# Half of the output projection moved from its own stage into the waits of the stage before it

## The reference, cut to what matters

```python
y = jnp.concatenate([gla_o, nsa_o], axis=-1) @ w_out      # 1024 x 1024
xp = xp + mod_p[:, 2] * yp                                # residual, gated
hp2 = modulate(xp, g_ffn, mod_p[:, 3], mod_p[:, 4])       # norm, scale, shift
f = moe_ffn(concat([hp2, hs2]), ...)                      # top 4 of 32 experts
y = rmsnorm(xp + mod_p[:, 5] * f, g_final)

def nsa_attend(q, ...):      # compressed, selected and window attention
    imp = sum of compressed softmax -> top_k blocks -> selected softmax
    return gates[0] * o_c + gates[1] * o_s + gates[2] * o_w
```

## Time and profile before

| | us |
|---|---|
| median of the runs | 1851.89 |
| the profiled execution's own time | 1850.02 |
| its span, first to last instruction | 1848.3 |
| sample attention, from barrier to barrier | 461.9 to 543.1 |
| output and router | 543.1 to 668.8 |
| experts and the end | 668.8 to 1848.3 |

### The profile page before, as it was taken

The page is one execution under the profiler, slowest core; times in us unless marked ns, Lnnn a source line. Parts: engine busy times, 40 slices in busy tenths (PEclk is TensorE's granted clock), DMA queues, the critical chain, the costliest instruction groups (busy, mean ns, idle before and its releaser), DMA issues.

```text
span 1848.3 us, 26967 instructions
## 1 busy us (share of the span) xinstructions
PE 1688.6 (91%) x9012; PEld 1314.5 (71%) x9012; DVE 1437.1 (78%) x1353; ACT 1102.1 (60%) x1049; POOL 332.4 (18%) x315
## 2 busy tenths in 40 slices
PE   4999777888779869999999999999999999999994
PEld 2777656555454547888888888888888888888873
DVE  4412464477433768999999999999999999999996
ACT  4221443355332346777777777777777777777772
POOL 0000112300001011222231231231231232222110
PEclk9999979799799869999999999999999999999997
DMA  9454373510046178999999999999999999999973
GB/s 348 167 201 147 82 232 115 168 39 2 14 150 183 64 297 293 356 369 379 374 376 377 377 370 375 380 371 371 387 376 369 388 369 377 384 374 369 388 290 122
DMA packets 112550, 516.08 MB, mean 279 GB/s; under 512 B 25678, under 2 KB 47518, under 8 KB 59754
## 3 DMA queue, kind: packets, MB, share of 16 engines
q1 hardware_dynamic: 99034, 483.48, 69.4%
q0 software_dynamic: 13456, 31.81, 6.1%
HBM read 502.75 MB, written 31.09 MB: 289 GB/s over the span
## 4 chain that ended last, share of the span: by engine, by line
PE 60%; DVE 2%; ACT 1%; DMA 1%; issue 0%; DVEq 0%; POOL 0%; ACTq 0%; POOLq 0%
PE banks L2764 56%; PE banks L2772 3%; PE banks L2750 1%; DMA ffn_rows<-weighed,block_rows 0%; DVE arena L3036 0%; DVE arena L3035 0%; ACT sigmoids L2937 0%; DVE split L2958 0%; PE banks L2822 0%; ACT split L2869 0%; DMA arena<-ffn_rows 0%; DVE arena L3054 0%; DVE split L2962 0%; DVEq L2631 0%; ACT final_stat L2938 0%
## 5 line engine op out<-in xcount | busy, mean ns | idle before, releaser
L2764 PE MATMUL banks<-split 128*128 128x512 f32 x4608 | 1080.0, 394 | 6.9 <-DVE split L2962 5.8
L2764 PEld LDWEIGHTS banks<-split 128*128 128x128 f32 x4608 | 863.3, 189 | 192.9 <-issue 13.7
L2958 DVE TENSOR_TENSOR split<-expert_buffers,split 128x2048 fp32r<-128x2048 f32 x384 | 864.8, 2285 | 44.3 <-ACT split L2869 42.8
L2869 ACT ACTIVATE split<-expert_buffers 128x2048 fp32r<-128x2048 f32 x384 | 733.2, 1918 | 223.6 <-PE banks L2764 216.6
L2703 POOL TENSOR_TENSOR wait_taken<-routing 128x1 f32<-128x1 f32 x62 | 76.1, 1227 | 815.2 <-PE banks L2772 464.4
L2726 POOL DMA_INDIRECT ffn_rows<-weighed,block_rows x31 | 107.7, 3474 | 4.8 <-issue 4.6
L526 PE MATMUL banks<-w_in_high,hT_high 128*128 128x476 f32 x192 | 75.4, 392 | 4.2 <-DVE hT_low L413 4.2
L439 DVE COPY arena<-banks 128x476 f32<-128x476 f32 x12 | 7.8, 654 | 91.1 <-PE banks L526 91.0
L2962 DVE TENSOR_TENSOR split<-banks,split 128x1024 fp32r<-128x1024 f32 x64 | 77.8, 1216 | 0.7 <-ACT split L2872 0.7
L526 PE MATMUL banks<-w_in_high,hT_low 128*128 128x476 f32 x192 | 73.1, 381 | 0.0
L2201 PE MATMUL banks<-arena 128*128 128x512 f32 (+1 forms) x160 | 66.9, 632 | 1.9 <-DMA arena<-in_w_out 1.9
(11 more groups left out here) (391 smaller groups left out, 1688.0 us busy)
## 6 DMA issues: line engine op xcount, KB each, us to landing
expert_buffers<-in_w_gate SPq DMA_DIRECT2D x128, 1024.0 KB, 8.2
expert_buffers<-in_w_up SPq DMA_DIRECT2D x128, 1024.0 KB, 5.9
expert_buffers<-in_w_down SPq DMA_DIRECT2D x128, 1024.0 KB, 9.5
arena<-in_w_ada SPq DMA_DIRECT2D x16, 1024.0 KB, 4.8
w_in_landing<-in_w_in SPq DMA_DIRECT2D x5, 1904.0 KB, 14.3
arena<-in_w_ada SPq DMA_DIRECT2D x4, 2048.0 KB, 22.1
arena<-in_x_prompt SPq DMA_DIRECT2D x8, 512.0 KB, 10.0
arena<-in_cache_cmp POOLq DMA_DIRECT2D x32, 128.0 KB, 3.5
```

The source lines that it names most:

```text
L2764: last = pe.matmul(ps[:, bank + c, :], x[:, kt * P:(kt + 1) * P].bitcast(F32R), wt.bitcast(F32R), start=(m == 2 and kt == 0 and x is xs[0] ...
L2869: act.activation(high[:, j % RING_Q].bitcast(F32R), v, ACT.Copy).then_inc(s_high, 1)
L2958: dve.tensor_tensor(rest[:, j % RING_Q].bitcast(F32R), v, high[:, j % RING_Q], ALU.subtract).then_inc(s_rest, 1)
```

## The change: what it does

Nothing of the arithmetic changes but where and in which order the output projection is computed. Its parts:

- In sample attention TensorE also turns the prompt's mixer rows, in eight groups of four transposes (`turn_mix(g)`), in bank F; ScalarE copies each group back over the rows it came from (`keep_turned(g)`).
- The left half of w_out (columns 0 to 511, 2 MB in 8 loads) is loaded at that stage's start. For each of the four prompt tiles TensorE computes the left half of the projection in two pieces of four slices (`left_half(t, 0, 4)`, `left_half(t, 4, 8)`) in bank F, and ScalarE keeps it in SBUF (`keep_left(t)`).
- The right half (2 MB in 2 loads) is loaded by SyncE in that stage once `values(1)` is done.
- In the output stage `project_out(t)` computes the right half only for the prompt's tiles; the sample tile has both halves there. VectorE's gating of a prompt tile is two operations of 512 columns, not one of 1024. The turning and copying of the prompt rows at its start is gone, and VectorE and ScalarE copy the turned sample rows before their first tile.
- ScalarE issues the stores of the first sums right behind its reads; GpSimd no longer does.
- In `experts`, `overflow` moves from behind `gate(1)` to behind `turn_rows(1)`.
- The sample tile's modulation vectors come in 16 loads, not 8, since their places are split up; other buffers move.

```diff
+    s_wo, s_turned, s_kept, s_yp, s_y = (core.sem(n) for n in (...))
@@ sample attention, SyncE
+            w_out = io["w_out"].rearrange("a (k p) n -> (a p) k n", p=P)
+            for kt in range(KT):
+                sp.dma_start(wout0[kt], w_out[:, kt, 0:512]).then_inc(s_wo, 16)
...
             for i in range(NU):
+                if i == 1:
+                    sp.wait_ge(s_pv, 2)
+                    for a, sem in enumerate(core.s_right):
+                        ks = slice(a * KT // 2, (a + 1) * KT // 2)
+                        sp.dma_start(wout1[:, ks, :], w_out[:, ks, 512:1024]).then_inc(sem, 16)
                 sp.wait_ge(s_res, i + 1)
@@ sample attention, ScalarE
+            def keep_turned(g):
+                t, a = divmod(g, 2)
+                act.wait_ge(s_turned, g + 1)
+                copy(mix[:, t, 512 * a:512 * (a + 1)], ps[:, F, :]).then_inc(s_kept, 1)
+            def keep_left(t):
+                act.wait_ge(s_yp, t + 1)
+                copy(y0[t], ps[:, F, :]).then_inc(s_y, 1)
             turn("k", 0)
+            keep_turned(0)
...
@@ sample attention, TensorE
+            def left_half(t, k0, k1):
+                if k0 == 0:
+                    pe.wait_ge(s_kept, 2 * ST)
+                    if t == 0:
+                        pe.wait_ge(s_wo, 16 * KT)
+                    else:
+                        pe.wait_ge(s_y, t)
+                for kt in range(k0, k1):
+                    last = pe.matmul(ps[:, F, :], mix[:, t, kt * P:(kt + 1) * P], wout0[kt], start=(kt == 0), stop=(kt == KT - 1))
...
+            scores(2)
+            left_half(0, 0, LEFT)
+            turn_weights(1)
+            left_half(0, LEFT, KT)
+            values(1)
+            left_half(1, 0, LEFT)
...
@@ output and router, TensorE
+            def project_out(t):
+                n = TILES[t][1]
                 if t >= 2:
                     pe.wait_ge(s_res, t - 1)
                 for kt in range(KT):
+                    if t == 0 and kt % (KT // 2) == 0:
+                        pe.wait_ge(core.s_right[kt // (KT // 2)], 16)
+                    if kt == KT // 2 and t >= 2:
+                        ranks(t - 2)
+                    right = wout1[:, kt, :]
+                    if t < ST:
+                        last = pe.matmul(ps[:, 4 + t % 2, :], mix[:, t, kt * P:(kt + 1) * P], right, start=(kt == 0), stop=(kt == KT - 1))
@@ output and router, ScalarE, in begin_read
+                act.wait_ge(s_bga, t + 1)
+                act.dma_start(core.ffn_d[t0:t0 + n, :], begin[t][0:n, :]).then_inc(core.s_begun if t else s_first_out, 16)
@@ output and router, VectorE
-                    link(dve.tensor_tensor(hh, ps[0:n, 4 + 2 * (t % 2):6 + 2 * (t % 2), :].rearrange("p b n -> p (b n)"),
-                                           ex[0:n, who, 0, :], ALU.mult))
+                    dve.tensor_tensor(hh[:, 0:512], y0[t], ex_out[0][:, 0:512], ALU.mult)
+                    link(dve.tensor_tensor(hh[:, 512:1024], ps[:, 4 + t % 2, :], ex_out[0][:, 512:1024], ALU.mult))
@@ experts, TensorE
             turn_rows(1, first=True)
+            overflow()
             def step(k, prev, last=False):
                 gate(k, first_of(prev))
-                if is_zero(prev):
-                    overflow()
                 turn_act(k)
```

More of the change, by code:

```diff
@@ L1646, in sample_attention @@
     CMP, IMP = 0, 3 * P
+    core.wout0, core.wout1, core.y0 = output_buffers(core)
+    wout0, wout1, y0 = core.wout0, core.wout1, core.y0
+    core.s_right = [core.sem(f"w_out_right_in{a}", carry=True) for a in range(2)]
+    LEFT = KT // 2
     rounds = [("k", 0, r) for r in range(6)] + [("k", 1, r) for r in range(6)]
@@ L1747, in _ @@
             last.then_inc(s_ec, 1)
+            def keep_turned(g):
[5 more added lines that the diff above has]
+                copy(y0[t], ps[:, F, :]).then_inc(s_y, 1)
             turn("k", 0)
+            keep_turned(0)
             window(0)
+            keep_turned(1)
             turn("k", 1)
+            keep_turned(2)
+            keep_turned(3)
+            keep_turned(4)
             exps(0)
-            for i in range(NU):
-                if i + 1 < NU:
-                    window(i + 1)
-                turn("p", i)
-                if i + 1 < NU:
-                    exps(i + 1)
-                if i + 2 < NU:
-                    turn("k", i + 2)
+            window(1)
+            turn("p", 0)
+            keep_turned(5)
+            exps(1)
+            turn("k", 2)
+            keep_turned(6)
+            keep_turned(7)
+            window(2)
+            turn("p", 1)
+            keep_left(0)
+            exps(2)
+            turn("k", 3)
+            keep_left(1)
+            window(3)
+            turn("p", 2)
+            keep_left(2)
+            exps(3)
+            turn("p", 3)
+            keep_left(3)
         @block.vector
@@ L1944, in _ @@
                       ).then_inc(s_imp, 1)
-            for i in range(NU):
-                if i + 1 < NU:
-                    scores(i + 1)
-                turn_weights(i)
-                if i + 2 < LATE:
-                    keys(i + 2)
-                values(i)
-                if LATE <= i + 2 < NU:
-                    keys(i + 2)
+            turn_mix(3)
+            turn_mix(4)
+            scores(1)
+            turn_weights(0)
+            turn_mix(5)
+            keys(2)
+            turn_mix(6)
+            values(0)
+            turn_mix(7)
+            scores(2)
[4 more added lines that the diff above has]
+            left_half(1, 0, LEFT)
+            keys(3)
+            left_half(1, LEFT, KT)
+            scores(3)
+            left_half(2, 0, LEFT)
+            turn_weights(2)
+            left_half(2, LEFT, KT)
+            values(2)
+            left_half(3, 0, LEFT)
+            turn_weights(3)
+            values(3)
+            left_half(3, LEFT, KT)
 def routing_tables(core):
@@ L2006, in output_and_router @@
     core.z_moe = own.at
-    mixT = own.take(KT * NTOK).rearrange("p (k n) -> p k n", k=KT)
-    wout = own.take(KT * D).rearrange("p (k n) -> p k n", k=KT)
+    own.take(KT * NTOK + KT * D)
+    hole = [core.pf + 2 * D + i * DIN + 512 for i in range(3)]
+    wout0, wout1, y0 = core.wout0, core.wout1, core.y0
+    mixST = mix[:, ST, 0:KT * (NTOK - SEQ)].rearrange("p (k n) -> p k n", k=KT)
     gate2 = core.gate2
@@ L2026, in output_and_router @@
     h2 = own.take(2 * D).rearrange("p (u n) -> p u n", u=2)
-    own = Stack(core, late.at, core.z1)
-    ex = own.take(6 * D).rearrange("p (w v n) -> p w v n", w=2, v=3)
+    own = Stack(core, late.at, core.z1 - 2 * PAST // PAGE * 256)
+    ex_out = [core.arena[:, hole[0] + 512:hole[0] + 512 + D], own.take(D)]
+    ex_ffn = [core.arena[:, at:at + 2 * D].rearrange("p (v n) -> p v n", v=2) for at in hole[1:3]]
     h2T = own.take(KT * P).rearrange("p (k n) -> p k n", k=KT)
@@ L2126, in _ @@
                     sp.wait_ge(s_yp, NT)
+                    sp.wait_ge(s_bp, 1)
                     for i in range(LANDING):
@@ L2162, in _ @@
             gather_rows(core, pool)
-            for t in range(2, NT):
-                store_begin(t)
             pool.wait_ge(s_bo, 16)
```

126 lines of the change are left out of this document (62 added, 64 removed).

## The result

Five runs of the changed kernel took 1833.33 to 1840.26 us, median **1835.73 us**; five of the kernel before, 1848.33 to 1853.65, median 1851.89. The ratio is 0.9924, 95% interval 0.9905 to 0.9943: 14 us less, between 10.6 and 17.6 (the two medians are 16.2 us apart). The profiled run's span went from 1848.3 to 1834.0 us.

A forecast was written before the change was run, and what follows sets the result against it. TensorE, busy 91% of the span, bounds the kernel; only waits, lower clock or movable work can give time. 19.7 - 28.6 - 1.0 - 2.3 = -12.2 us, from 1851.89 to a median of 1839.7; 8 in 10: 1829 to 1853.

The forecast's parts named there:

- the likeliest case: Whole kernel: the forecast itself, a median of 1839.7 us within 1834 to 1845, chance 0.58.
- sample attention: Sample attention: added pieces and transposes, partly in TensorE's holes, start the next stage +19.7 us later, bounds +14 and +26.
- output stage to the sample tile: Output stage up to VectorE's start on the sample tile: halved projections give -28.6 us, bounds -32.5 and -9.
- tail: End of the output stage: ScalarE's stores replace GpSimd's before the barrier, -1 us, bounds +1 and -4.
- `overflow`: Experts' stage: moved, it starts in a hole of 2.38 us and delays the gate by 2.3: -2.3 us.
- The forecast's 4.3: Sample attention from 504.73 to the stage's end: holes the left-half pieces fill, 4.3 us, bounds 0 and 9.
- The 1 us of clock that I gave `scores(1)`: Sample attention: a shorter hole before `scores(1)` may let it keep more of the clock, 1 us.
- 2 us for dips: Output stage: low-clock dips in the projection pieces cost 2 us in all; first-piece dips hide behind the ranks' wait.
- the first rival: Output stage: right halves run at 1.2 GHz throughout, gain only -9.3 us, 1859.0 us in all; chance 0.10.
- one dip in two: Output stage: after the same light stretch, the clock falls in one projection of two, as at 0.61 and 1.00 before.
- The first branch of the prediction's bound: Barrier behind the output stage: if GpSimd's own DMAs cause its 6.2 us, up to 4 us go.
- my bound of -4.6: Experts' stage: the lower bound for moving `overflow`, which took 4.6 us between the gate's and next products.

The follow-up runs named there:

- experiment 3: The kernel before with only `overflow` moved to behind turn_rows(1): 1847.67 us, ratio 0.9975.
- experiment 4: The kernel before with only the stores of the first sums issued by ScalarE: 1847.36 us, ratio 0.9979.
- experiment 5: The changed kernel with all eight left-half pieces behind values(3), at the end of sample attention: 1844.15 us, ratio 0.9964.
- experiment 8: The changed kernel without the eight left-half pieces in sample attention, ScalarE's copies kept: one profiled run, 1818.65 us, no ratio.
- experiment 7: The changed kernel with two more GpSimd fills directly in front of its gather: one profiled run, 1837.31 us, no ratio.
- experiment 1: The changed kernel with `overflow` put back behind the second gate: 1842.54 us, ratio 0.9948.
- experiment 10: The changed kernel with ranks behind the projection, rows turned inside it, left halves of tiles 1 to 3 gated by GpSimd, experts' gates loaded later: 1834.66 us, ratio 0.9899.
- experiment 2: The changed kernel with GpSimd storing the first sums again: 1841.09 us, ratio 0.9932.
- experiment 6: The changed kernel with ranks(t-2) behind the last product of project_out(t), not in its middle: 1838.27 us, ratio 0.9941.
- experiment 11: The kernel of experiment 10 with the load of the router's biases issued second, not tenth, in the output stage: 1835.76 us, ratio 0.9918.

## Why the prediction was right

Forecast 1839.7 us, measured 1835.73, inside the likeliest case's own 1834 to 1845. By its steps, against the two single profiles:

| step | forecast | the two profiles | medians of the forms |
|---|---|---|---|
| sample attention | +19.7 | +18.6 | +21.3 |
| output stage to the sample tile | -28.6 | -27.2 | -26.0 |
| tail | -1 | -2.0 | -2.6 |
| `overflow` | -2.3 | -5.1 | -4.3 |
| sum | -12.2 | -15.7, and 1.4 back, a later start of the stage | -11.6 |

The last column has the median over all profiles in whose kernels that stage is of the one form or the other (3 and 8 for A, 3 and 6 for B, 3 and 9 for C, 3 and 10 for D). It says more than one pair of profiles, since the changed kernel's own profile has the shortest A of the eight (99.4 us, the others 101.8 to 102.3) and one of the short Bs. By it the projection's move (the first two steps) gained 4.7 us where I had 8.9, and the two small parts gained 6.9 where I had 3.3. The sum came right in part by luck: two errors of about 4 us stood against each other. No run has the move alone. An estimate from the ratios, 0.9924 divided by 0.9975 and 0.9979 (experiments 3 and 4), is 0.997: 5.6 us less, with some 5 us of uncertainty either way.

- *Sample attention.* The mechanism was right: the pieces fill the waits that stand behind them, nothing waits for `keep_left`, and the stage's end is no longer SyncE's (experiments 5, 8). From `scores(2)` to the last piece TensorE takes 55.4 us in the changed kernel and 31.35 to the end of `values(3)` in experiment 8, so the 27.6 us cost 24.1: the pieces filled holes worth 3.5 us. The forecast's 4.3 was against the kernel before, where the same stretch took 32.5; against that it is 4.7, and 1.2 of it, part of the DMA wait of 2.12 us, had gone without the pieces (0.94 in experiment 8, none in 5). The 1 us of clock that I gave `scores(1)` came in one profile of eight; in the others `scores(1)` stays slow throughout (5.6 to 5.7 us), and so does some of what follows, down to the start of `values(0)`. That is the spread from 99.4 to 102.3. The kernel before had `scores(1)` at 4.6 us in experiments 3 and 4; the profile that I forecast from, with 5.7, was the slow one of three. So `scores(2)` starts 1.4 to 1.9 us later in the other seven than in that profile, where I had 0.5 earlier: this is the most of what +19.7 lacks to +21.3.
- *Output stage.* `project_out(0)` 8.56 us (forecast 8.6), `turn_rows(0)` at 18.0 (18.5), a tile 14.4 (13.8), from tile 3's end to the sample tile 15.1 (15.1). Tile 2 ended at 32.3, not 29.6: its router products and first piece were slow (3.62 and 5.20 us where full speed is 1.97 and 3.7). I had 2 us for dips; 3.3 came on TensorE.
- *Tile 2, and a wait that I put at nothing.* VectorE may start on tile 2 only when the store of tile 0's rows has landed. SyncE issued it 18.7 us into the stage (581.8), it landed at 33.1, and VectorE started at 33.3, 0.7 us later than TensorE allowed (in tile 3 it starts 0.3 us behind TensorE). So without any dip in tile 2 VectorE would still have started at 33.3, if the store landed as it did, and my 2 us for dips covered the most of it by luck. In five of the six profiles with this output stage VectorE starts 0.2 us behind the landing, at 33.0 to 35.8; in experiment 7 the store landed at 31.4, and VectorE started with TensorE at 32.9. From that start to the sample tile it is 28.5 us in four of the six and 30.0 and 30.2 in experiments 5 and 1, which had a slow second piece. These two things are the spread of B from 61.4 to 65.3. The loads in front of the store are not separated: 9 loads of the experts' gates stand there, and in experiment 10, which moved them, it still took 14.2 us to land for 14.5, though only 1.25 us behind the last load of the experts' biases, not 4.2. No run moves the store alone.
- *The clock, against the first rival.* I said one dip in two; it is nearly one in every tile (15 of 18 first pieces in the six profiles). Yet the mean clock of the stretch was 0.87, far from the 0.65 at which the rival decides, because the dip ends within the first piece, and in tile 3 it costs nothing: `take_rank(0)` starts 9.4 us behind VectorE's start on tile 2 in all six profiles, so with the piece at full clock the ranks wait longer (2.96 us in experiment 8). A dip in the second piece does cost, 1.5 to 1.7 us, and came in two of six profiles. The Trainium skill's page "TensorE: Matmul & The Clock Gate", section "A second HAM failure mode: psum-queue depth-cycling", was right about the swings (0.70 then 1.00, 0.75 then 1.00); the price was small since VectorE, and the store that it waits for, set the tiles, not TensorE.
- *Tail.* The first branch of the prediction's bound was right: GpSimd's own DMA holds the barrier up (experiments 2, 4, 7). The gain is 2.0 to 2.7 us, not 1 and not the bound's 4, because the gather is GpSimd's too and now holds the barrier.
- *`overflow`* is the term that I mis-sized most. I counted what lies in the hole of 2.38 us and left out what the hole did to the products behind it, 13.98 us for 12.61. Of the 5.1 us 1.0 was chance, the rest is `overflow`'s: 4.1 by the rows, 4.3 by the medians (experiments 1, 3), near my bound of -4.6.

The two forecasts on waits: that for `take_rank` came with 1.38 and 0.72 us, not 2.4, for the slow piece in front of it took the rest. The wait for the store of tile 0's rows was not in the forecast.

## What to carry to other kernels

Independent products put directly in front of an instruction that is known to wait are nearly free for the length of that wait, and they can also save what the products behind it lose at the lower clock (2.4 and 1.4 us at `overflow`), so price a hole with both. When the heavy engine's part of a pipelined tile is halved, add up the other engine's chain for one tile first: it is the new bound (12.3 us here), together with what that chain waits for, the landing of an earlier tile's store included. Dips of the heavy engine that end before it cost nothing, and curing its waits brings only what lies above that chain (in experiment 6 1.4 us from VectorE's start on tile 2 to the sample tile). Behind a barrier look at which engine's DMA is issued last, not only at which instruction ends last.

## What the runs showed of the hardware

- The barrier of the output stage comes some 6 us behind the end of GpSimd's last DMA issue (5.9 to 6.8 us in all 14 profiles, store or gather), that of sample attention 2.2 us behind SyncE's where SyncE ends the stage (540.92 to 543.16 before) and 1.95 us behind ScalarE's copy where that does (561.19 to 563.14 in the changed kernel). Why was not tried. Where GpSimd's last DMA is a store (before, experiments 2 and 3), the next stage starts 1.4 us behind its landing; ScalarE's last store in the changed kernel landed at 660.24, 0.65 us after the next stage had started. That would fit a barrier that waits for the landing of GpSimd's DMAs and not of ScalarE's; no run here tries it.
- GpSimd and VectorE slowed each other in experiments 10 and 11. GpSimd's operation of 128x512 takes 1.26 us alone and 2.27 beside VectorE; VectorE's of 128x1024 with both inputs in SBUF 2.17 in place of 1.22, while the one with an input in a bank kept its 0.68. The first to start kept its length too (VectorE's 1.28 at 579.45):

```profile
571.98 1.26 POOL L2233 TENSOR_TENSOR arena<-arena 128x512 f32<-128x512 f32 x1 [5.45 <-DMA arena<-modulation]
...
579.59 2.27 POOL L2235 TENSOR_TENSOR arena<-arena 128x512 f32<-128x512 f32 x1 [6.34 <-DMA arena<-in_x_prompt]
```
```profile
579.45 1.28 DVE L2559 SCALAR_TENSOR_TENSOR arena<-arena 128x1024 f32<-128x1024 f32 x1
580.77 2.17 DVE L2561 TENSOR_TENSOR arena<-arena 128x1024 f32<-128x1024 f32 x1
582.86 0.68 DVE L2547 TENSOR_TENSOR arena<-banks,arena 128x512 f32<-128x512 f32 x1
```

The Trainium skill's page "GPSIMD Engine Reference", section "1. Specifications", says that GpSimd shares its way to SBUF with VectorE and contends with operations of two SBUF inputs; the rows agree. Here it delayed the norm of tile 0 and so `turn_rows(0)` by 1 us, part of what experiment 10 lost.
- After 4 us of transposes, router products and a wait of 1.2 us TensorE's next products began at 1.2 GHz in nearly every tile (5.20, 5.38 and 5.27 us for a piece that takes 3.7 at 2.4 GHz), but not in all: 3.68 us in experiments 5 and 8 for the same instructions of tile 3, and 3.65 in experiment 1 for those of tile 4.
